# Turned-around router product, GpSimd for the low parts and two early expert loads in a fused two-block transformer kernel

## The reference, cut to what matters

```python
x = x + mod_x[:, 2, None] * mx
hx = modulate(rms_norm(x, g_ffn[layer]), mod_x[:, 3], mod_x[:, 4])

def expert_choice_ffn(h, w_router, w_gate, w_up, w_down):      # h is (1, 512, 1024), w_router (1024, 16)
    aff = jax.nn.softmax((h @ w_router).astype(jnp.float32), axis=-1)
    gate, idx = lax.top_k(jnp.swapaxes(aff, 1, 2), cap)         # cap = 64, per expert over the tokens
    xe = h[bidx, idx]
    hid = jax.nn.silu(einsum('becd,edf->becf', xe, w_gate)) * einsum('becd,edf->becf', xe, w_up)
    ye = einsum('becf,efd->becd', hid, w_down) * gate[..., None]
    return zeros_like(h).at[bidx, idx].add(ye)
```

## Time and profile before

| quantity | value |
|---|---|
| median of 3 runs | 3108.59 us (3106.37 to 3109.65) |
| the profiled execution, its own time | 3108.51 us |
| its span, first to last instruction | 3106.7 us |
| mean granted TensorE clock | 0.945 of full speed |
| TensorE matmul busy | 2868.7 us, 92% |
| DVE, ACT, POOL busy | 973.2, 895.4, 635.5 us |
| DMA moved | 424.70 MB |

### The profile page before, as it was taken

One profiled execution on the slowest core, in us unless ns is written; L12 is line 12 of the kernel. 1 busy time (PEld: TensorE's weight loads), 2 busy tenths in 40 slices (PEclk: granted clock), 3 DMA queues, 4 the chain that ended last, 5 costly groups with the idle time before them and its releaser, 6 DMA issues.

```text
span 3106.7 us, 37266 instructions
## 1 busy us (share of the span) xinstructions
PE 2868.7 (92%) x15332; PEld 2147.9 (69%) x15332; DVE 973.2 (31%) x1429; ACT 895.4 (29%) x1360; POOL 635.5 (20%) x319
## 2 busy tenths in 40 slices
PE   5899899999969999998999999899998889998997
PEld 3756677688744343337799667899997778566886
DVE  3322420611242111113266353311134065542213
ACT  4122333432321111103332333311133243343223
POOL 1211012044400000001221000622222222006443
PEclk6999999999979999998999899999997988999999
DMA  5143204022358999993121101111132122002222
GB/s 243 42 158 146 109 15 149 1 93 97 124 212 364 422 422 422 422 422 138 60 95 43 65 1 75 60 63 67 56 108 109 54 97 80 31 1 106 104 95 95
DMA packets 64783, 424.70 MB, mean 137 GB/s; under 512 B 6848, under 2 KB 6848, under 8 KB 18176
## 3 DMA queue, kind: packets, MB, share of 16 engines
q1 hardware_dynamic: 52416, 375.41, 30.7%
q0 software_dynamic: 3808, 27.81, 2.3%
q10 hardware_dynamic: 8416, 19.40, 1.7%
HBM read 405.56 MB, written 17.04 MB: 136 GB/s over the span
## 4 chain that ended last, share of the span: by engine, by line
PE 78%; DMA 9%; DVE 5%; ACT 4%; POOL 2%; issue 2%; ACTq 0%; SPq 0%; DVEq 0%; POOLq 0%
PE psum L669 74%; DMA ring<-in_weights 5%; PE psum L672 3%; DMA late_slots<-in_weights 2%; DMA arena<-in_t_count 1%; ACT hidden_high L1562 1%; POOL weight_parts L2768 1%; ACT arena L1571 1%; POOL arena L2854 1%; DVE small L2095 1%; ACT hidden L1556 0%; ACT arena L1593 0%; DVE arena L2528 0%; POOL arena L2860 0%; DVE merged_low L2157 0%
## 5 line engine op out<-in xcount | busy, mean ns | idle before, releaser
L669 PE MATMUL psum<-hidden_high,weight_parts 128*128 128x384 f32 (+2 forms) x3296 | 881.0, 368 | 55.1 <-DVE hidden_low L2048 20.8
L2768 POOL TENSOR_TENSOR weight_parts<-ring,weight_parts 128x1024 fp32r<-128x1024 f32 x218 | 537.6, 2468 | 1399.0 <-ACT weight_parts L1526 1378.0
L669 PEld LDWEIGHTS psum<-hidden_high,weight_parts 128*128 128x128 f32 x3296 | 617.3, 194 | 135.8 <-issue 37.4
L669 PE MATMUL psum<-hidden_low,weight_parts 128*128 128x384 f32 (+2 forms) x2160 | 660.7, 366 | 4.9 <-DVE merged_low L2157 4.9
L1526 ACT ACTIVATE weight_parts<-ring 128x1024 fp32r<-128x1024 f32 x218 | 230.6, 1061 | 1113.8 <-PE psum L669 1109.8
L669 PE MATMUL psum<-arena 128*64 128x128 f32 (+8 forms) x3120 | 523.5, 370 | 15.0 <-DMA arena<-in_weights 6.5
L669 PEld LDWEIGHTS psum<-hidden_low,weight_parts 128*128 128x128 f32 x2160 | 407.5, 193 | 45.0 <-DVE merged_low L2157 6.3
L669 PEld LDWEIGHTS psum<-arena 128*64 128x64 f32 (+3 forms) x3120 | 296.4, 161 | 182.3 <-issue 136.9
L1571 ACT ACTIVATE arena<-psum 128x512 f32<-128x512 f32 (+4 forms) x225 | 159.9, 720 | 407.9 <-PE psum L669 390.3
L2175 DVE TENSOR_TENSOR arena<-arena,psum 128x512 f32<-128x512 f32 (+1 forms) x72 | 55.9, 777 | 521.9 <-PE psum L669 521.1
L669 PE MATMUL psum<-ring,arena 128*64 128x512 f32 (+1 forms) x792 | 193.4, 600 | 14.6 <-DMA ring<-in_weights 12.9
(11 more groups left out here) (283 smaller groups left out, 2417.5 us busy)
## 6 DMA issues: line engine op xcount, KB each, us to landing
ring<-in_weights SPq DMA_DIRECT2D x260, 1024.0 KB, 6.8
late_slots<-in_weights SPq DMA_DIRECT2D x48, 1024.0 KB, 15.3
arena<-in_weights SPq DMA_DIRECT2D x48, 1024.0 KB, 17.4
spilled_projections<-arena ACTq DMA_DIRECT2D x14, 384.0 KB, 2.3
arena<-spilled_projections ACTq DMA_DIRECT2D x3, 1536.0 KB, 13.5
residual<-in_acts POOLq DMA_DIRECT2D x1, 3072.0 KB, 19.9
arena<-in_bias POOLq DMA_DIRECT2D x1, 3072.0 KB, 10.6
arena<-in_t_count POOLq DMA_DIRECT2D x2, 1536.0 KB, 11.5
```

Source lines behind the costliest of these rows:

```text
L669: return nc.tensor.matmul(o, lhsT, rhs, start=start, stop=stop)
L2768: G_.tensor_tensor(parts[:, i % 2, 1, :], tile_at(t), parts[:, i % 2, 0, :], ALU.subtract).then_inc(*E.sig("tile_split"))
```

## The change

- `eWR` moves from the arena to `small`, which grows by 128 columns (the arena shrinks by as many), and GpSimd issues its load much earlier, behind the load of the neighbourhood bias.
- The router product is turned around: `eWR[:, k, :]` (128x16) is the stationary side, and 512 tokens stream, in 8 matmuls into one group `logits` (16x512). VectorE copies it to SBUF, and four transposes bring it back to the old layout.
- On TensorE block (1,0) moves from behind the router to behind HT 3; affT now comes after HT 1 instead of HT 2.
- ScalarE copies each turned tile twice (`eHi`, and a plain copy `eTurned`) and frees the PSUM region; the low part is taken by GpSimd from SBUF (`turned_low`), and the first gather waits for that.
- SP loads `e0` and `e0+1` ahead of block (1,2).

```diff
-ARENA = 53184 - 2 * KT * TOK - NSLOT * UNIT - 4096 - NPAR - NCONST - 520
+ARENA = 53184 - 2 * KT * TOK - NSLOT * UNIT - 4096 - NPAR - NCONST - 648
...
-        eWR = split(area(XP + 20480, 128), a=KT)
+        eWR = split(small[:, 520:648], a=KT)
+        eTurned = [area(XP + at, 1024) for at in (14336, 16384, 17408, 19456)]
... TensorE
-            ps = [group("router", n) for n in range(2)]
+            ps = group("logits")
             for k in range(KT):
                 pe.wait_ge(*E.next("ffn_hidden_ready"))
-                for tt in range(4):
-                    at = (tt % 2) * 512
-                    ins = mm(ps[tt // 2][:, at:at + NE], H3[:, k, CTX + tt * P:CTX + (tt + 1) * P], eWR[:, k, :],
-                             k == 0, k == KT - 1)
-                    refill(ins)
-                    if k == KT - 1 and tt % 2:
-                        ins.then_inc(psum_full, 1)
-
-            modulation_sums(("mod2", 1), 0, cond2)
+                ins = mm(ps[0:NE, 0:512], eWR[:, k, :], H3[:, k, CTX:TOK], k == 0, k == KT - 1)
+                refill(ins)
+            ins.then_inc(psum_full, 1)
+            pe.wait_ge(*E.taken("logits"))
+            for n in range(2):
+                ps = group("router", n)
+                for i in range(2):
+                    tt = 2 * n + i
+                    ins = flip(ps[:, i * 512:i * 512 + NE], eW[0:NE, 1, tt * P:(tt + 1) * P])
+                ins.then_inc(psum_full, 1)
...
-            for tt in range(3):
+            for tt in range(2):
                 hidden_turn(tt)
...
-            hidden_turn(3)
+            for tt in range(2, 4):
+                hidden_turn(tt)
+            modulation_sums(("mod2", 1), 0, cond2)
             modulation_turn(("mod2", 0), 2)
...
-                pe.wait_ge(*E.taken("HT", tt))
+                pe.wait_ge(*E.next("turned_low"))
... ScalarE
-            modulation_rows(("mod2", 1), 0)
             for tt in range(4):
                 act.wait_ge(*E.written("HT", tt))
                 act_(eHi[:, tt, :], cols("HT", tt), ACT.Copy).then_inc(*E.sig("turned_high"))
+                act_(eTurned[tt], cols("HT", tt), ACT.Copy).then_inc(*E.read("HT", tt))
+            modulation_rows(("mod2", 1), 0)
... VectorE
-            def turned_low(tt):
-                dve.wait_ge(*E.next("turned_high"))
-                tt_(eLo[:, tt, :], cols("HT", tt), eHi[:, tt, :], ALU.subtract).then_inc(*E.read("HT", tt))
-
+            dve.wait_ge(*E.written("logits"))
+            V.tensor_copy(eW[0:NE, 1, :], cols("logits")[0:NE, 0:512]).then_inc(*E.read("logits"))
...
-            for tt in range(3):
-                turned_low(tt)
             dve.wait_ge(*E.written("affT"))
...
-            turned_low(3)
... GpSimd
             pool.dma_start(nB, split(dram["bias"], h=8)).then_inc(sem("bias_loaded"), 16)
+            pool.dma_start(eWR, dram["router"]).then_inc(sem("router_loaded"), 16)
...
-            pool.dma_start(eWR, dram["router"]).then_inc(sem("router_loaded"), 16)
+            for tt in range(4):
+                pool.wait_ge(*E.next("turned_high"))
+                pool.wait_ge(*E.taken("HT", tt))
+                G_.tensor_tensor(eLo[:, tt, :], eTurned[tt], eHi[:, tt, :], ALU.subtract)\
+                    .then_inc(*E.sig("turned_low"))
... SP
-            in_turn(NSLOT, e0)
+            in_turn(NSLOT, e0 - NSLOT)
             sp.wait_ge(sem("ffn_hidden_ready"), 1)
             for i in range(2):
                 load(e0 + i, expert_order[i])
+            in_turn(e0 - NSLOT, e0)
```

More of the change, by code:

```diff
@@ L321, in program @@
         arena_parts = ctx.enter_context(nc.sbuf_tensor("arena_parts", [P, ARENA], f32r))
-        small = sbuf("small", 520)
+        small = sbuf("small", 648)
         psum = ctx.enter_context(nc.psum_tensor("psum", [P, 8 * 512], f32))
```

## The result

| | before | after |
|---|---|---|
| median of the runs made together | 3107.48 us (4 runs, 3106.32 to 3109.65) | 3085.68 us (4 runs, 3084.05 to 3088.13) |
| the profiled execution, its own time | 3108.51 us | 3088.13 us |
| its span | 3106.7 us | 3086.3 us |
| mean granted TensorE clock | 0.945 | 0.951 |

The ratio is 0.993, 95% interval 0.9912 to 0.9947: **21.8 us faster**, between 16.5 and 27.3. The forecast was 3092.3 with a range of 3087 to 3100. The direction is right; the time lies 1.3 us under the range's low end.

What follows compares the result with a forecast made beforehand. One serial line over five engines was taken to set when the expert layer, itself bound by its weight stream, starts. Legs 6.5 + 6.7 + 6.8, less 4.6 wait, plus 0.8 gather, gave 16.2 us: 3108.5 to 3092.3, range 3087 to 3100.

Steps and rivals of the forecast that it cites:

- Router weights early: Ahead of the router: loading its weights far earlier removes TensorE's wait after block (0,2), 6.5 us to 0.
- Turned product: Router product on TensorE: 16 records of 512 streamed columns take 7.1 us at full clock, against 13.8 before.
- The rival of a low clock: Clock stays low in the router, which ends at 891.2: gain only 8.5 to 9.5 us, 3099.5 us; chance 0.12.
- From the router to MAX8: Router's end to the first top-k step: copy, transposes, softmax chain and affT take 6.5 us against 13.3.
- What is late next: Before pos: the weights of block (1,2) become the limit; the top-k is ready 4.8 us before pos starts at 911.0.
- the new wait: Pos waiting for block (1,2) after the top-k would be ready: 4.6 us subtracted in the sum.
- the start of (1,2)'s loads: Block (1,0) starts at 894.5; the first load of (1,2) is issued 2.9 us later, at 897.4.
- that second case: Block (1,0) at full clock: first load of (1,2) issued after 1.5 us, and pos at 909.5.
- Gather: Gather after pos, 6.47 us before at half clock: 0.8 us gained from a higher clock, bounds 0 and 2.5.
- GpSimd's low parts: Four subtractions of 2.4 us each on GpSimd, done by 902 and hidden by 11 us before the gather.
- the rival that GpSimd holds VectorE up: Each of four GpSimd subtractions stops VectorE for 2.4 us, top-k ends at 915.8: gain 11.5, 3097 us; chance 0.08.
- the three legs: Wait ahead of the router, router product, and router to MAX8: gains of 6.5, 6.7 and 6.8 us.

Runs made afterwards that it cites:

- the padded kernel: The changed kernel with 25 further chained MAX8 of unused result between pos and the one-hots: 4.0 us faster than the kernel before (0.6 to 7.5), ratio 0.9987.
- The runs of comparison and placement: The kernel before unedited against itself, and the kernel before with only the buffer placement changed (`small` 128 columns more, arena 128 fewer): ratio 0.9998 each.
- the early and turned router: The kernel before with router weights loaded early and the product turned around; low parts, order and queues as before: 19.3 us faster, ratio 0.9938.

## Why the prediction came out as it did

**Router weights early: right.** 6.5 us were expected and the idle time of 6.55 is gone; alone it gave 8.8 in the stage; what goes beyond 6.5 is the clock of the product and of the gather, less a slower block (1,0).

**Turned product: right.** 7.1 expected, 7.03 measured in all ten profiles that have it, at the full clock. The rival of a low clock fell: the earlier trace rows had shown the half clock where TensorE waited and then ran the old form, and the run without the turned product shows that the old form loses the clock by itself.

**From the router to MAX8: right.** 6.5 us expected, 6.3 measured (882.85 to 889.17).

**What is late next: the mechanism right, its size wrong.** This is the term of the stage's sum that failed: 4.6 us for the new wait, and 2.9 measured. Told from the router's start, the top-k was to be ready after 29.0 us and pos to start after 33.8, a wait of 4.8 (4.6 in the sum, which counts from the old pos). The run with block (1,0) first confirms the 29.0; pos came after 31.9 (31.8 to 32.5 in the three other profiles of this kernel), so the wait is 2.9 us. The step behind it that failed is the start of (1,2)'s loads. Block (1,0) began after 16.1 us and not 17.3: ScalarE was free 0.3 us sooner; its four copies took 3.8 us and not 4.1, since they follow each other every 0.91 us though each lasts 1.03 (887.10, 888.01, 888.91, 889.81); and HT 3 took 1.0 us in front of the block at full clock, where I had 1.6. The block itself ran at full clock, 3.63 us and not 4.9, so its first load went out 1.5 us behind its start and not 2.9. I had named that second case as a bound and not taken it. The first weights, 5.1 us behind their issue and not 4.8, thus came after 22.7 us instead of 25.0. From there to pos it was 9.2 us, where I had 8.8.

**Gather: no gain.** 0.8 us of gain expected; 6.74 measured against 6.47, so 0.3 lost, and 6.62 in another profile. That is just outside my bounds of 0 and 2.5, and the upper one was out of reach, as the 4.56 us at full clock show. Block (1,2), broken by waits (TensorE busy 1.1 to 1.4 us of every 2 from 900 to 906), did not hold the clock up to it: the granted clock is 0.50 from 900 to 916.

**GpSimd's low parts: right.** 2.36 us each against 2.4, done by 898.6, hidden. VectorE beside them was not slowed: MAX8 0.68 us, as before. So the rival that GpSimd holds VectorE up fell. The rows from which I took that GpSimd gives way could not have told: in them VectorE's instruction had started first (842.16 against 842.31). The rule of the Trainium skill, "SBUF — State Buffer", section "Who interferes with whom", is about VectorE instructions with two SBUF inputs, and it says that one with at most one, outside the two-port modes, does not contend with GpSimd. MAX8 has one input of 16x512 here, and the trace agrees: 0.68 us beside GpSimd as without it. What two-input instructions would lose behind GpSimd, no run here shows.

**The sum.** 6.5 + 6.8 + 7.0 for the three legs, less 2.9 and less 0.3, is 17.1 us; the stage shows 17.4 in the first pair of profiles and 17.5 over all (68.7 less 51.2). Forecast: 16.2. The stage accounts for 1.3 us of the miss of 6.6. The two errors in it, 1.7 us on the wait and 1.1 on the gather, have opposite signs, so that the sum came out close is in part luck. My own range was also added up wrongly: pos at 909.5 with 2.5 us from the gather, and pos at 912.3 with none, give 3089.1 and 3094.4, where the prediction has 3089.5 and 3095.5.

**The rest: a term put at nothing.** The step that put the time below the range is the one that counted nothing outside the stage. The median of before stood 1.1 us lower in this comparison than in the runs shown (3107.48 against 3108.59). Some 4 us remain, which the sum had put at zero: it took everything outside the stage as unchanged, and the range was made from terms of the stage alone. On other chips the same kernel had medians of 3090.31 and 3089.17 us, inside the range, with gains of 22.1 and 20.2. So a part goes with the scatter of the granted clock between executions. The earlier trace rows could have warned me of it: they show both of its levels within 12 us. A part, 0.6 to 7.5 us by the padded kernel, does not go with the stage's length. A place where it may arise is seen (ahead of 286 us, 2.3 us on average between the old and the new order), its cause isn't. The runs of comparison and placement show no effect (0.6 us, -2.5 to 3.7), which leaves room for a small one; the early and turned router has an excess of 5.2 us without the new order and with a late memset, so that place is not the whole of it. Whether the clock truly falls less often on identical instructions, and why, stays open.

**A better version.** Block (1,0) ahead of the last two turned tiles takes the wait away: 0.992 and 0.9921 against 0.993, 0.9929 and 0.9935 for the change, and on one chip 3083.89 us against 3090.31. The intervals overlap; the stage, 46.8 us on average against 51.2, says the same.

## What to carry to other kernels

When a serial line over several engines is shortened, look for the next late thing among the loads that the shortened line itself triggers, and count when their first issue goes out; then the remaining edits overlap (up to pos the turned product was worth 5.9 us where the top-k was the limit and 2.7 in the full change). Put the instruction block whose end releases loads as early as its data allows. And in a range of some 0.2%, allow for what the clock does in stretches that nobody edited: here 8.4 us in four profiles of one kernel.

## What the runs showed of the hardware

- The same product in two forms treats the clock differently. In the 64 weight loads of 128x128 with 16 columns behind each, the granted clock fell from 2.4 to 1.2 GHz (1.00, 0.65, 0.50 in three windows of 2 us) with TensorE busy 2.00 us of each; in the 16 records of 512 columns over a 16-column stationary side, at the same place, it stayed at 2.4 (1.00 from 876 to 884 us), and the product took 7.03 us against 10.30.
- Two executions of identical instructions differ by 3.8 us within the first 286 us; what their windows show beside that is the granted clock, low in two more places. Sixteen profiles fall into the same two kinds: 0.81 to 0.82 over 169 to 178 and 205 to 214 us in the eleven late ones, 1.00 in the five early ones.
- The gather of 16 records took between 4.56 and 6.74 us in different profiles: the same work at full clock (4.56, in part waiting for VectorE) and at half (6.70).
